# Starting a recurrence's preparation inside the attention before it, and casting single weight slabs early at nine places of a three-block transformer kernel

## The reference

```python
z = z + mu * (z_prev - z)                       # token shift, 15 tiles here
r, k, v, w_lo, a_lo, g_lo = _split(z, RWKV_SPLITS)
w = -softplus(-(w0 + tanh(w_lo) @ w2)) - 0.5    # rank 64
a = sigmoid(a0 + a_lo @ a2)                     # rank 64
g = sigmoid(g_lo) @ g2                          # rank 160
kk = (k * k_k) / max(norm of (k * k_k) per head, 1e-12)
k = k * (1 + (a - 1) * k_a);  decay = exp(-exp(w));  b = kk * a
# then 512 steps of: state = state*decay + (state @ -kk) b + v k;  y = state @ r
bonus = sum(r * k * r_k) * v;  y = (groupnorm(y) * ln_w + ln_b + bonus) * g
```

## Time and profile before

| | |
|---|---|
| three timed runs | 3088.44, 3088.87, 3089.86 us (median 3088.87) |
| the profiled execution | 3085.53 us, its span 3083.7 us |
| busy | PE 2916.3 (95%), DVE 1262.2 (41%), ACT 1149.0 (37%), POOL 1496.0 (49%) |
| TensorE's granted clock over the span | 0.977 |

### The profile page before, as it was taken

The page is one execution under the profiler, slowest core; times in us unless marked ns, Lnnn a source line. Parts: engine busy times, 40 slices in busy tenths (PEclk is TensorE's granted clock), DMA queues, the critical chain, the costliest instruction groups (busy, mean ns, idle before and its releaser), DMA issues.

```text
span 3083.7 us, 41172 instructions
## 1 busy us (share of the span) xinstructions
PE 2916.3 (95%) x15600; PEld 2298.2 (75%) x15600; DVE 1262.2 (41%) x2023; ACT 1149.0 (37%) x1678; POOL 1496.0 (49%) x1883
## 2 busy tenths in 40 slices
PE   7999969899999998999999999989998887999998
PEld 6777648788888885867888887757777676888886
DVE  4066474554211645142362225151475633562222
ACT  4534533443222427234342224243544424442222
POOL 5445502256555674536565554515226324665553
PEclk9999989999999999999999999989999899999999
DMA  4323200233333332325322222312112103422222
GB/s 138 103 90 93 66 1 3 88 118 97 99 93 96 134 104 86 109 69 195 124 95 96 96 96 89 122 45 89 65 59 84 53 26 134 169 94 96 96 96 82
DMA packets 80673, 284.16 MB, mean 92 GB/s; under 512 B 8968, under 2 KB 9096, under 8 KB 79744
## 3 DMA queue, kind: packets, MB, share of 16 engines
q1 hardware_dynamic: 66240, 236.36, 23.3%
q10 hardware_dynamic: 13296, 41.97, 3.6%
q0 software_dynamic: 976, 3.56, 0.4%
HBM read 260.86 MB, written 20.99 MB: 91 GB/s over the span
## 4 chain that ended last, share of the span: by engine, by line
PE 41%; issue 27%; POOL 25%; DVE 3%; ACT 2%; DMA 0%; POOLq 0%; ACTq 0%; SPq 0%; DVEq 0%
POOL slab_r L2988 25%; PE bank L366 11%; PE bank L368 10%; PE bank L367 10%; PE bank L615 2%; PE bank L592 1%; PE bank L686 1%; PE bank L734 1%; PE bank L499 1%; PE bank L509 1%; PE bank L991 0%; PE bank L673 0%; PE bank L1096 0%; PE bank L795 0%; ACT slab_high L1241 0%
## 5 line engine op out<-in xcount | busy, mean ns | idle before, releaser
L2988 POOL TENSOR_TENSOR slab_r<-slab,slab_high 128x256 fp32r<-128x256 f32 x1768 | 1397.0, 822 | 1352.9 <-ACT slab_high L1241 1346.1
L366 PE MATMUL bank<-xh,slab_high 128*128 128x512 f32 x2256 | 909.0, 403 | 31.8 <-POOL slab_r L2988 26.6
L368 PE MATMUL bank<-xh,slab_r 128*128 128x512 f32 x2256 | 884.7, 392 | 0.0
L367 PE MATMUL bank<-x_raw_r,slab_high 128*128 128x512 f32 x2064 | 810.4, 393 | 0.0
L1241 ACT CAST slab_high<-slab 128x1024 fp32r<-128x1024 f32 x442 | 462.1, 1046 | 450.0 <-DMA slab<-in_w_down 216.4
L367 PE MATMUL bank<-work_r,slab_high 128*128 128x512 f32 x1376 | 543.0, 395 | 0.0
L366 PEld LDWEIGHTS bank<-xh,slab_high 128*128 128x128 f32 x2256 | 428.0, 190 | 151.3 <-POOL slab_r L2988 32.4
L368 PEld LDWEIGHTS bank<-xh,slab_r 128*128 128x128 f32 x2256 | 427.5, 189 | 93.0
L366 PE MATMUL bank<-work_r,slab_high 128*128 128x512 f32 x1184 | 469.2, 396 | 23.5 <-DMA cst<-in_cst 15.9
L368 PE MATMUL bank<-work_r,slab_r 128*128 128x512 f32 x1184 | 471.5, 398 | 0.0
L367 PEld LDWEIGHTS bank<-x_raw_r,slab_high 128*128 128x128 f32 x2064 | 391.9, 190 | 81.1 <-issue 3.3
(11 more groups left out here) (463 smaller groups left out, 2714.5 us busy)
## 6 DMA issues: line engine op xcount, KB each, us to landing
slab<-in_w_down SPq DMA_DIRECT2D x88, 512.0 KB, 3.5
slab<-in_w_up SPq DMA_DIRECT2D x64, 512.0 KB, 3.5
slab<-in_w_gates SPq DMA_DIRECT2D x56, 512.0 KB, 3.5
slab<-in_w_merge SPq DMA_DIRECT2D x48, 512.0 KB, 4.1
slab<-in_w_gu SPq DMA_DIRECT2D x44, 512.0 KB, 3.5
slab<-in_w_in_a SPq DMA_DIRECT2D x32, 512.0 KB, 3.5
gates<-staging ACTq DMA_DIRECT2D x56, 256.0 KB, 3.9
slab<-in_w_out SPq DMA_DIRECT2D x24, 512.0 KB, 3.5
```

Source lines behind the costliest of these rows:

```text
L366: first = pe.matmul(bank[b][:, :], wh, mh, start=start, stop=False)
L367: pe.matmul(bank[b][:, :], wh, ml, start=False, stop=False)
L368: end = pe.matmul(bank[b][:, :], wl, mh, start=False, stop=stop)
L2988: low = pool.tensor_tensor(slab_low[:, slot, at], slab[:, slot, at], plain(slab_high[:, slot, at]), ALU.subtract)
```

## The change

Two things. First, work of the recurrence's preparation moves into and around the attention's end. The shift takes tile 28 (inputs of the rank-64 products) and the key tiles first; the key scale runs on DVE in the steps 21 to 24, the tanh on ACT in step 20; the rank-64 products of tiles 0 and 1 run on PE in the steps 30 and 31, those of 2 and 3 behind the attention; their sigmoids come first on ACT, and DVE does its four scans ahead of the key sums' evictions. The rank-160 products and their copies come last. Second, `high_ahead` casts the next slab at a chosen place, and the next `high_turn` (the new name of `high_next`) then casts none. It stands at nine places. The copies of in_d are unrolled with a cast before each, and the wait for `h_used` moves from before the first to before the ninth.

```diff
-        shift_tiles = list(range(16, 30)) + [31]
+        shift_tiles = [28] + list(range(20, 24)) + list(range(16, 20)) + list(range(24, 28)) + [29, 31]
+        KEYS_FROM, HIDDEN_AT, RATES_AT = 21, 20, (30, 31)
+        RATE_BANKS, KEY_BANKS = (0, 4, 0, 4), (6, 7, 2, 3)
...
+            def rates(c):                                  # PE
+                s = slice(c * P, (c + 1) * P)
+                for e in range(2):
+                    b, r = RATE_BANKS[c] + e, slice(e * HD, (e + 1) * HD)
+                    if last[b]:
+                        pe.wait_ge(*last[b])
+                    pe.matmul(bank[b][:, :], W(LOW_RANK[0])[r, s], W(28)[r, :], start=True, stop=True)\
+                        .then_inc(psum_for["act_beside"], hand(b, "act_beside"))
...
                     early_gates(IN_ATTENTION)
+                    if g in RATES_AT:
...
+                        rates(RATES_AT.index(g))
                     turn_probs(g)
...
+            mark("key_sums")
+            for c in (2, 3):
+                rates(c)
+            for c in range(4):
+                sum_tiles([W(SQUARES + c)], KEY_BANKS[c], "dve", pair, S("kk_square"))
+            pe.wait_ge(S("lora_ready"), n.next(S("lora_ready"), 2))
...
+            ahead = [0]                                    # ACT
+            def high_turn():
+                if ahead[0]:
+                    ahead[0] -= 1
+                    return
+                if to_split[0] < total_slabs:
+                    high_part(to_split[0])
+                to_split[0] += 1
+            def high_ahead():
+                high_part(to_split[0])
+                to_split[0] += 1
+                ahead[0] += 1
...
             for g in range(len(steps) + 2):
                 if g < len(steps):
                     exps(g)
-                elif g == len(steps):
-                    key_squares()
+                if g == HIDDEN_AT:
...
+                if g == len(steps):
+                    for c in range(2):
+                        rates(c)
...
+            for c in (2, 3):
+                rates(c)
             send_gates(0, AFTER_ATTENTION)
...
                 act.wait_ge(S("norm_square"), n.next(S("norm_square")))
                 act.activation(W(41 + c), W(41 + c), ACT.Sqrt).then_inc(S("lru_norm"), n.up(S("lru_norm")))
+                if c in (2, 6):
+                    high_ahead()
...
-            act.wait_ge(S("h_used"), n.next(S("h_used")))
-            copy_tiles("in_d", FIRST_D, W3(0, FIRST_D))
+            for t in range(FIRST_D):
+                high_turn()
+                if t == DC:
+                    act.wait_ge(S("h_used"), n.next(S("h_used")))
+                act.wait_ge(psum_for["act"], d0 + t + 1)
+                act.copy(W(t), bank[t % RING][:, :]).then_inc(evac, 1)
...
+            for c in range(4):                             # DVE
+                decay_scan(c)
+            for c in range(4):
+                dve.wait_ge(psum_for["dve"], n.next(psum_for["dve"]))
+                dve.tensor_scalar(W(SQUARES + c), bank[KEY_BANKS[c]][:, :], 1e-24, 2.0 ** 30, ALU.max, ALU.mult)\
+                    .then_inc(evac, n.up(evac))
+            for c in range(4):
+                decay_sums(c)
```

More of the change, by code:

```diff
@@ L745, in _ @@
                     values(g - 1)
-            mark("rwkv")
-            def low_rank(c):
-                s = slice(c * P, (c + 1) * P)
[L753 to L774, removed]
+            mark("key_sums")
[5 more added lines that the diff above has]
+            for c in range(4):
+                s = slice(c * P, (c + 1) * P)
+                if last[c]:
+                    pe.wait_ge(*last[c])
+                pe.matmul(bank[c][:, :], W(LOW_RANK[1])[:, s], W(29), start=True, stop=False)
+                pe.matmul(bank[c][:, :], W(LOW_RANK[2])[0:32, s], W(31)[0:32, :], start=False, stop=True)\
+                    .then_inc(psum_for["act"], hand(c, "act"))
             for c in range(4):
@@ L1241, in high_part @@
                 act.copy(slab_high[:, slot, :], slab[:, slot, :]).then_inc(S("slab_high"), 1)
+            ahead = [0]
[10 more added lines that the diff above has]
+                ahead[0] += 1
             def steps_of(stage, n_slabs, body=None, peel=False):
+                assert not ahead[0], stage
                 s0 = to_split[0]
@@ L1565, in _ @@
                     exps(g)
-                elif g == len(steps):
-                    key_squares()
+                if g == HIDDEN_AT:
+                    act.wait_ge(S("shift_done"), n.next(S("shift_done")))
+                    act.activation(W(28)[0:HD, :], W(28)[0:HD, :], ACT.Tanh)\
+                        .then_inc(S("lora_ready"), n.up(S("lora_ready")))
+                if g == len(steps):
+                    for c in range(2):
+                        rates(c)
                 if 1 <= g <= len(steps):
@@ L1589, in _ @@
                 act.activation(W(SQUARES + c), W(SQUARES + c), ACT.Ln).then_inc(chain, n.up(chain))
-                act.wait_ge(chain, n.own(chain))
+            act.wait_ge(chain, n.own(chain))
             for c in range(4):
@@ L1608, in _ @@
             act.wait_ge(S("decays_ready"), n.own(S("decays_ready")))
+            for c in range(4):
+                act.wait_ge(psum_for["act"], n.next(psum_for["act"]))
+                act.copy(W(36 + c), bank[c][:, :]).then_inc(evac, n.up(evac))
             def pack_blocks(sources, packed, heads):
@@ L1912, in _ @@
                     floor_copy(h + 1)
+                if h == 1:
+                    high_ahead()
                 if h < 2:
@@ L2451, in _, with decay_scan @@
             dve.wait_ge(chain, n.own(chain))
-            for c in range(4):
-                dve.wait_ge(psum_for["dve"], n.next(psum_for["dve"]))
-                dve.tensor_scalar(W(SQUARES + c), bank[4 + c][:, :], 1e-24, 2.0 ** 30, ALU.max, ALU.mult)\
-                    .then_inc(evac, n.up(evac))
-            for c in range(4):
-                dve.wait_ge(evac_by["act"], handed_at["rwkv"]["act"] + 3 * c + 2)
+            w3 = lambda i: W(i).rearrange("p (n t) -> p n t", n=NT)
+            def decay_scan(c):
+                dve.wait_ge(evac_by["act_beside"], 2 * c + 1)
                 for t in range(NT):
```

104 lines of the change are left out of this document (56 added, 48 removed).

## The result

The changed kernel took 3067.75 us, the median of four runs (3065.58 to 3071.73), against 3088.65 us for the kernel before beside it (four runs, 3087.44 to 3089.86). The ratio is 0.993, with a 95% interval of 0.9914 to 0.9946: 17 to 27 us faster. The forecast was 3065, the range 3056 to 3078. The profiled execution took 3065.58 us, its span 3063.8 against 3083.7: 19.9 us less, where my sum had 24.0. The page after has PE at 2917.9 us (95%), ACT at 1145.3, DVE at 1266.9 and POOL at 1507.6.

A forecast was written before the change was run, and what follows sets the result against it. PE, 95% busy, was the bound, idle at the recurrence's preparation and late ACT casts. 7.3 + 8.8 + 5.0 + 0 + 1.8 + 1.5 + 1.5 - 1.9 = 24.0 us off 3088.9 gave 3065 us, range 3056 to 3078.

The forecast's parts named there:

- Seam: Recurrence's preparation after the attention: operands begin at 406.9 instead of 414.19, 7.3 us won, bounds 4 and 9.
- in_d: Slab cast ahead of Exp, later casts not waiting for h_used: 6.85 idle plus 1.95 slow restart, 8.8 us won.
- Delta rule's norm and merge: Last norm: 4.33 idle plus 1.7 slow restart less 1.05, 5.0 us; following merge: wait moves to a bank, 0.
- Merge in block two: The 1.53 us of idle PE goes, with PE the bound behind it: 1.5 us won.
- RG-LRU: Wait at 1217 goes, but PE idles some 6 us before 1247.2 with slow restart: -1.9 us, bounds -4 and +1.
- GLA: Softplus: PE's 5.07 us slab wait goes, but ACT's first-level exp stands behind: 1.8 us won, bounds 0.5 and 3.
- the first term of the sum: GLA's softplus: two casts leave ACT's path, one enters, second transposes then wait about 0.6; 1.3 us won.
- The second term: GLA's softplus: 0.5 us won from a DVE that no longer runs beside POOL.
- mLSTM: Cast moves ahead of decays, a DVE row comes 1.03 later; 3.84 idle before, 1.5 us won, bounds 0 and 4.5.
- The chain that I named: mLSTM: reciprocal, products and next weights soon hold PE instead of the slab, leaving a gain of 1.5 us.
- where the idle time goes, that goes too: Slow restart after long idle, priced at in_d: half clock for some 4 us, 1.95 us lost, vanishing with the gap.
- the rivals: Preparation only, 3081.6 (0.06); half, 12 us (0.17); nearly all, 34.5 us (0.12); casts stalling on landings, 3112 (0.02); no change (0.03).

The follow-up runs named there:

- Experiment 5: Changed kernel with ScalarE's wait for h_used put back in front of in_d's loop, the cast ahead kept; one run, 3071.06 us.
- experiment 3: Changed kernel with more uv slabs cast ahead in the RG-LRU instead of two: four took 3065.52 us, three 3071.22 us (one run).
- experiment 4: Changed kernel with GLA's second cast later: 3067.27 us; plus three uv slabs and mLSTM cast moved: 3062.03; gate copies moved too: 3060.91.

## Why the prediction was right, and where not

- *Seam, 7.3 forecast, 6.1 measured.* The order of events was as I followed it: evictions done at 387.4 (387.0 forecast), keys from 392.7 (392.4) to 405.5 (405.0), no wait for the Exp, no PE wait in the steps 30 and 31. The operands began at 407.78 (406.9), which is 6.4 won: the keys ended 0.5 late, the last sum took 2.05 us (I took 1.9), and 0.2 are gaps. The idle time fell by 6.9, and the low clock cost 0.7 more.
- *in_d, 8.8 forecast, 9.0 measured.* The idle time fell by 6.85 and the low clock's cost by 1.98 (1.95 forecast). Experiment 5 splits it.
- *Delta rule's norm and merge, 5.0 and 0 forecast, 6.6 and -1.35 measured.* Together 5.3. The idle time fell by 5.1 at the norm, and the merge's two waits became one of the same sum, as worked out; the rest is the clock's, 1.46 won and 1.71 lost. That part is luck of the trace: of the twelve traces with these casts eight have the norm's stretch at 43.4 to 43.5 us and four at 46.5 to 48.5.
- *Merge in block two, 1.5 and 1.8.* PE was the bound behind it.
- *RG-LRU, -1.9 and -1.8.* The wait moved to the slab behind DVE's chain: 6.15 us, "some 6" forecast. What I did not see is that the fifth tile lacks a bank as well as a slab (experiment 3); it changed nothing here, as the slab came last. Right too was that the chain's end would stay, since as many splits lay beside it; experiment 3 shows what each costs, 1.5 us.
- *GLA, 1.8 and 1.0.* The idle time fell by 1.3, the first term of the sum, and the low clock cost 0.4 more. The second term, 0.5 "from a DVE that no longer runs beside POOL", did not come. That step was wrong: with the second cast behind the Ln, POOL's part moved on top of the scans and made them 1.46 us longer. It had stood clear of them before. But undoing this gave PE 0.3 us at most, and with the gate copies gone as well the wait was still 4.89 (experiment 4): what holds it is the chain from DVE's differences over ACT's table load and exponentials.
- *mLSTM, 1.5 forecast, -1.6 measured, the step that failed.* The chain that I named did come to hold PE, and the idle time fell by 1.3 of the 1.5. What I left out was the clock, though I had priced it at in_d: "where the idle time goes, that goes too". Here it did not go. The gap left was 2.80 us instead of 3.84, and the time at 1.2 GHz behind it cost 4.84 us, not 1.71. With two gaps of 0.7 us it cost nothing. Why a gap of 2.8 us in front of the products of L979 is followed by more low clock than one of 3.8 in front of a slab's is not shown.
- *Unforecast:* the scans between 2330 and 2500 lost 1.1 and the end won 0.9, both in the low clock, which varies there between executions by as much.

Of the rivals, none came: none of the ten casts ahead waited for a landing, and the 20.9 us by the medians are nearer to 24 than to 12. The range held by a wide margin, but single sites missed by up to 3.1 us and in part cancelled.

## What to carry to other kernels

Before moving an operation into another engine's idle time, ask for three things in the trace: what is queued behind it (here an Abs with no slack), what its product sets off and beside which work that will lie (here POOL's split beside DVE's scans), and where the wait will be found afterwards. When effects of a tenth of a per cent are at stake, align the matmuls of two traces and compare idle time by stretch: over the whole program it differed by 0.6 and 1.7 us in the two kernels that were traced twice, where the times of the same kernel differ by six. Take a second trace before a difference under 2 us is believed. Count the clock as its own term, in both directions: a shorter gap can cost more than a longer one (the mLSTM), and removing one can give more than its length (in_d, 9.0 us for 6.85).

## What the runs showed of the hardware that I had not expected

- PE's clock: in the mLSTM a gap of 2.80 us went with 4.8 to 4.9 us lost at 1.2 GHz in every trace that has it (seven), gaps of 3.84 and 2.46 in front of a slab's products with 1.7 (three traces; 2.46 with the preparation alone), two of 0.7 with none (four). In the RG-LRU's stretch a gap of 6.15 us went with 1.5 to 2.3, one of 4.88 with 2.9 and one of 3.4 with 1.6 to 2.8. The loss does not follow the length of the gap.
- The same instructions in the same order lost between 1.6 and 8.2 us to the low clock in one stretch that no edit touched. The runs of the kernel before span 3082.98 to 3094.28 us on one chip. Idle time and this loss trade in part: the stretch from 2000 to 2105 had 10.3 us idle and 7.8 lost before, and 7.2 idle and 15.2 lost with the preparation alone.
- DVE and POOL: beside POOL's splits a DVE product of two 128x512 tiles takes 1.05 us instead of 0.69 and a scan 1.65 instead of 1.23, while POOL takes 1.28 us an instruction instead of 0.71.
